# A fused decoder layer in one core: the up projection of blocks 1 to 3, hidden chunks 4 to 15, as seven half-size products instead of eight

## The reference, cut to what matters

```
def sq_relu_mlp(h, w_up, w_down):
    u = jax.nn.relu(h @ w_up)
    return (u * u) @ w_down
...
x = x + sq_relu_mlp(rms_norm(x, norm_mlp[i]), w_up[i], w_down[i])
return rms_norm(x, final_norm)
```

## Time and profile before

| | us |
|---|---|
| median of 3 runs | 2531.71 (2530.8 to 2531.89) |
| span of the profiled execution (first to last instruction) | 2527.2 |
| what the median is above that span | 4.5 |
| TensorE busy in the span | 2490.0 (99%) |
| VectorE busy | 1691.7 (67%) |
| ScalarE busy | 1247.7 (49%) |

### The profile page before, as it was taken

One profiled execution on the slowest core, in us unless ns is written; L12 is line 12 of the kernel. 1 busy time (PEld: TensorE's weight loads), 2 busy tenths in 40 slices (PEclk: granted clock), 3 DMA queues, 4 the chain that ended last, 5 costly groups with the idle time before them and its releaser, 6 DMA issues.

```text
span 2527.2 us, 31134 instructions
## 1 busy us (share of the span) xinstructions
PE 2490.0 (99%) x11724; PEld 2087.1 (83%) x11724; DVE 1691.7 (67%) x2473; ACT 1247.7 (49%) x1832; POOL 345.9 (14%) x328
## 2 busy tenths in 40 slices
PE   8999999999999999999999999999999999999998
PEld 7888887888788888888888888888888888888887
DVE  5677467566767786665566778656665687765566
ACT  5544354544554455455455445545455445554344
POOL 0034200000304320000110431000020143000000
PEclk9999999999999999999999999999999999999999
DMA  8522458555732143544442215354444213443443
GB/s 292 183 84 67 157 194 304 182 205 171 261 134 67 51 175 117 190 144 133 166 168 82 67 56 203 100 183 150 150 167 147 70 59 107 160 134 120 164 150 133
DMA packets 201681, 369.48 MB, mean 146 GB/s; under 512 B 8032, under 2 KB 120032, under 8 KB 192576
## 3 DMA queue, kind: packets, MB, share of 16 engines
q1 hardware_dynamic: 200912, 367.25, 43.0%
q10 hardware_dynamic: 624, 0.27, 0.0%
HBM read 336.03 MB, written 31.46 MB: 145 GB/s over the span
## 4 chain that ended last, share of the span: by engine, by line
PE 86%; DVE 5%; DMA 3%; ACT 2%; issue 2%; POOL 1%; DVEq 0%; SPq 0%; ACTq 0%; POOLq 0%
PE banks L2174 25%; PE banks L2175 25%; PE banks L2176 25%; PE banks L2348 3%; POOL queries L946 1%; PE banks L2387 1%; PE banks L2391 1%; PE banks L2327 1%; DVE w_lo L1527 1%; PE banks L2372 1%; PE banks L2304 1%; DMA xres<-in_x 1%; DMA raw<-w_out_mix 1%; DVE xres L1928 0%; DVE query_dec L1679 0%
## 5 line engine op out<-in xcount | busy, mean ns | idle before, releaser
L2174 PE MATMUL banks<-h_hi,w_hi 128*128 128x512 f32 (+1 forms) x1728 | 666.5, 386 | 3.3 <-issue 1.3
L2176 PE MATMUL banks<-h_hi,w_lo 128*128 128x512 f32 (+1 forms) x1728 | 659.0, 381 | 0.0
L2175 PE MATMUL banks<-h_lo,w_hi 128*128 128x512 f32 (+1 forms) x1728 | 659.0, 381 | 0.0
L1527 DVE TENSOR_TENSOR w_lo<-raw,w_hi 128x1024 fp32r<-128x1024 f32 x284 | 357.6, 1294 | 105.2 <-ACT w_hi L1030 97.6
L1520 DVE TENSOR_TENSOR w_lo<-raw,w_hi 128x2048 fp32r<-128x2048 f32 x122 | 292.6, 2398 | 149.2 <-ACT w_hi L1023 145.4
L1030 ACT ACTIVATE w_hi<-raw 128x1024 fp32r<-128x1024 f32 x248 | 253.9, 1053 | 279.3 <-PE banks L2174 93.0
L2174 PEld LDWEIGHTS banks<-h_hi,w_hi 128*128 128x128 f32 x1728 | 324.9, 188 | 66.2 <-issue 4.8
L2176 PEld LDWEIGHTS banks<-h_hi,w_lo 128*128 128x128 f32 x1728 | 324.8, 188 | 63.3
L2175 PEld LDWEIGHTS banks<-h_lo,w_hi 128*128 128x128 f32 x1728 | 325.0, 188 | 60.9
L2174 PE MATMUL banks<-w_hi,u_hi 128*128 128x512 f32 x896 | 350.9, 392 | 2.3 <-DVE w_lo L1527 1.8
L2176 PE MATMUL banks<-w_hi,u_lo 128*128 128x512 f32 x896 | 349.4, 390 | 0.0
(11 more groups left out here) (237 smaller groups left out, 3485.7 us busy)
## 6 DMA issues: line engine op xcount, KB each, us to landing
raw<-in_w_up SPq DMA_DIRECT2D x64, 1024.0 KB, 5.7
raw<-w_mix SPq DMA_DIRECT2D x64, 1024.0 KB, 4.7
raw<-in_gla_w_in SPq DMA_DIRECT2D x56, 1024.0 KB, 5.1
raw<-in_w_down SPq DMA_DIRECT2D x48, 1024.0 KB, 5.1
raw<-w_out_mix SPq DMA_DIRECT2D x24, 512.0 KB, 4.3
raw<-in_w_out SPq DMA_DIRECT2D x21, 512.0 KB, 3.7
xin<-in_w_down SPq DMA_DIRECT2D x10, 1024.0 KB, 5.1
w_mix<-xin SPq DMA_DIRECT2D x10, 1024.0 KB, 5.3
```

The lines of the kernel that those rows point to most:

```text
L1527: nc.vector.tensor_tensor(w_lo[:, i % 2, at], raw[:, i % 2, at], w_hi[:, i % 2, at].bitcast(F32), ALU.subtract).then_inc(lo_split.sem, 1)
L2174: after_chunk(pe.matmul(to, left[0], right[0], start=start, stop=False, skip_group_check=goes_on))
L2175: pe.matmul(to, left[0], right[1], start=False, stop=False, skip_group_check=goes_on)
L2176: return pe.matmul(to, left[1], right[0], start=False, stop=stop, skip_group_check=goes_on)
```

## The change

Block 0 keeps the order `MLP`. Blocks 1 to 3 get a list of their own, `LATE_MLP`: U0 to U3, down 0, U4 to U7, down 1, U8 to U11, down 2, U12 to U15, down 3. U0 to U3 (`PLAIN_UPS`) stay as they were; each of U4 to U15 becomes seven products of 4 blocks x 3 matmuls with 256 moving columns, issued as two steps, "up a" and "up b":

```
+LATE_UP_A = (("M1", A11, 0), ("M2", A12, 1), ("M6", S2, 2), ("M5", S1, 3))
+LATE_UP_B = (("M7", S3, 1), ("M3", S4, 0), ("M4", A22, 2))
+for _g in range(GROUPS):
+    for _c in range(DEPTH * _g, DEPTH * (_g + 1)):
+        LATE_MLP += [("up", _c)] if _c < PLAIN_UPS else [("up a", _c), ("up b", _c)]
+    LATE_MLP += [("down", _g, j) for j in range(len(PRODUCTS))]
+def late_bank(c, name):
+    return {"M2": 6, "M5": 1, "M3": 1}.get(name, 7 if c % 2 else 0)
```

TensorE. M1, M6, M7 and M4 of a chunk go on in one bank and M5, M3 in another, and ScalarE (`keep_part`) or VectorE (`add_part`) has to take the sum so far before the next product writes there:

```
+def late_up(s, c):
+    pe.wait_ge(*up_split_loaded[a % 2].at(n, late_parts_before(s)))
+    late_products(s, c, "M1", "M2")
...
+    wait_piece(s, 0)
+    late_products(s, c, "M6")
+    wait_piece(s, 1)
+    late_products(s, c, "M5")
...
+    wait_piece(s + 1, 0)
+    late_products(s + 1, c, "M7")
...
+    late_products(s + 1, c, "M3")
...
+    late_products(s + 1, c, "M4")
+# in late_products, before each product's 12 matmuls:
+        pe.wait_ge(*empty(n, ("up", c, name)))
```

ScalarE, in blocks 1 to 3 (its order for one late chunk, and at the start of a down group):

```
+def late_up(s, c):
+    if ahead is not None:
+        late_body(ahead)
+        corner(ahead)
+    keep_part(c, "M1")
+    if ahead is not None:
+        u_high(ahead, False)
+    late_split_hi(s + 1, 0) 
+    late_split_hi(s + 1, 1)
+    keep_part(c, "M6")
+    if ahead is not None:
+        u_high(ahead, True)
+    keep_part(c, "M5")
+    late_split_hi(s + 2, 0)
+    late_split_hi(s + 2, 1)
+    late_relu(c)
+def late_down(s, g, j):
+        late_body(c)
+        corner(c)
+        late_split_hi(s + 1, 0)
+        u_high(c, False)
...
```

VectorE, the same way:

```
+def late_up(s, c):
+        u_sums(ahead)
+    add_part(c, "M2")
+    late_split_lo(s + 1, 0)
+    late_split_lo(s + 1, 1)
+        u_low(ahead, False)
+        u_low(ahead, True)
+    add_part(c, "M7")
+    late_split_lo(s + 2, 0)
+    add_part(c, "M3")
+    late_split_lo(s + 2, 1)
+def late_down(s, g, j):
+        u_sums(c)
+        late_split_lo(s + 1, 0)
+        u_low(c, False)
+        late_split_lo(s + 1, 1)
+        u_low(c, True)
```

Block 0 makes what the late chunks load. For each of its up chunks 4 to 15, VectorE makes four sums of 512 columns (`up_mix`: four instructions, behind the split of that chunk), and SyncE stores them and the split weights that the late chunks use unchanged:

```
+def up_mix_store(c):
+    sp.wait_ge(up_mix_made, c - PLAIN_UPS + 1)
+    sp.dma_start(w_up_mix[:, c - PLAIN_UPS, 0:2, :], up_mix_t2_t1)
+    sp.dma_start(w_up_mix[:, c - PLAIN_UPS, 2:4, :], up_mix_t3_t4)
+def up_split_store(i, c):
+    for part, high_low in enumerate((w_hi, w_lo)):
...
...
+                    if s >= 2 and MLP[s - 2][0] == "up" and MLP[s - 2][1] >= PLAIN_UPS:
+                        up_mix_store(MLP[s - 2][1])
                     load(n, c_mlp + s, *mlp_source(s))
+                    if s >= 2 and MLP[s - 2][0] == "up" and MLP[s - 2][1] >= PLAIN_UPS:
+                        up_split_store(c_mlp + s - 2, MLP[s - 2][1])
...
+                        act.wait_ge(up_split_stored[slot], 64 * stored_ups(slot, s - 1))
```

More of the change, by code:

```diff
@@ L248, in block_uses @@
         yield from output_uses()
-    for what in MLP:
+    for what in MLP if plain else LATE_MLP:
         if what[0] == "up":
@@ L252, in block_uses @@
                 yield f, ("up", what[1], f)
+        elif what[0] in ("up a", "up b"):
+            for name, _, _ in LATE_UP_A if what[0] == "up a" else LATE_UP_B:
+                yield late_bank(what[1], name), ("up", what[1], name)
         else:
@@ L334, in __init__ @@
         self.mlp = C_OUT + out_chunks
-        self.chunks = self.mlp + len(MLP)
+        self.steps = MLP if plain else LATE_MLP
+        self.chunks = self.mlp + len(self.steps)
         self.uses = UseOrder(block_uses(plain))
@@ L717, in mlp_source, with late_weights, late_columns, stored_ups @@
             return wdown[:, 2 * DEPTH * g + row:2 * DEPTH * (g + 1):2, 512 * col:512 * (col + 1)], DEPTH
+        def late_weights(s):
+            what = LATE_MLP[s]
+            if what[0] == "up":
+                return wup[:, :, FCOLS * what[1]:FCOLS * (what[1] + 1)], KD
+            g, operand = what[1], PRODUCTS[what[2]][2]
+            if operand >= T1:
+                return w_mix[:, g, operand - T1, :, :], DEPTH
+            row, col = {B11: (0, 0), B21: (1, 0), B22: (1, 1)}[operand]
+            return wdown[:, 2 * DEPTH * g + row:2 * DEPTH * (g + 1):2, 512 * col:512 * (col + 1)], DEPTH
+        def late_columns(s, piece):
+            first = {"up a": 1024, "up b": 512}.get(LATE_MLP[s][0])
+            return slice(1024 * piece, 1024 * (piece + 1)) if first is None else \
+                slice(first + 512 * piece, first + 512 * (piece + 1))
+        def stored_ups(slot, steps):
+            return sum(MLP[t][0] == "up" and MLP[t][1] >= PLAIN_UPS and (FIRST.mlp + t) % 2 == slot for t in range(steps))
+        def late_parity(s):
+            return (OTHERS.mlp + s) % 2
+        def late_parts_before(s):
+            return sum(LATE_MLP[t][0] in ("up a", "up b") and late_parity(t) == late_parity(s) for t in range(s))
+        def ring(n):
+            return LATE_RING if n else RING
         def chunk_source(i):
@@ new lines, in first_mlp @@
+                            finish_u(after_up)
+                        if g == 1 and 1 <= j <= TILES:
+                            if j == 1:
+                                act.wait_ge(*xin_loaded.at(n, 0))
+                            square(1, j - 1, xin, n)
+                        if g == GROUPS - 1:
+                            if j == 0:
+                                act.wait_ge(*full(n, "next rstd"))
+                                nc.scalar.activation(rstd_rows, bank("next rstd"), ACT.Copy)\
+                                    .then_inc(bank_read[bank_of("next rstd")], 1)
+                            for k in NEXT_X_TILES.get(j, ()):
+                                next_x_high(k)
+                            if j == len(PRODUCTS) - 1:
+                                for t in range(2):
+                                    act.wait_ge(*read(n, ("down", g, "M2", t)))
+                                    square(2, t, xres, n)
@@ L1476, in _ @@
+                if n:
+                    late_mlp()
+                else:
+                    first_mlp()
                 for t in range(2, TILES):
@@ new lines, in first_mlp, with late_split_lo @@
+                        if g == GROUPS - 1:
+                            for k in NEXT_X_TILES.get(j, ()):
+                                next_x_low(k)
+                            if j == len(PRODUCTS) - 1:
+                                for t in range(2):
+                                    norm_ms(2, t)
+                def late_split_lo(s, piece):
+                    i, what = c_mlp + s, LATE_MLP[s]
+                    dve.wait_ge(*hi_split.at(n, PIECES * i + piece))
+                    at = late_columns(s, piece)
+                    nc.vector.tensor_tensor(w_lo[:, i % 2, at], raw[:, i % 2, at], w_hi[:, i % 2, at].bitcast(F32),
+                                            ALU.subtract).then_inc(lo_split.sem, 1)
@@ L2113, in final_scale, with late_mlp @@
+                def late_mlp():
+                    for s, what in enumerate(LATE_MLP):
+                        if what[0] == "up":
+                            plain_up(s, what[1])
+                        elif what[0] == "up a":
+                            late_up(s, what[1])
+                        elif what[0] == "down":
+                            late_down(s, *what[1:])
+                if n:
+                    late_mlp()
+                else:
+                    first_mlp()
                 def final_scale(t):
@@ L2689, in pe_block @@
                 first_up_chunk()
-                for s, what in enumerate(MLP):
+                for s, what in enumerate(mlp_steps):
                     if what[0] == "up":
```

567 lines of the change are left out of this document (435 added, 132 removed).

## The result

| | before | after |
|---|---|---|
| median of the runs, us | 2531.57 | 2553.73 (2552.59 to 2554.46) |
| span of the profiled execution, us | 2527.2 | 2550.8 |

The changed kernel is slower: 1.0089 times before, 95% interval 1.0075 to 1.0103, +22.2 us. The prediction had 2521.6 us in a range of 2510 to 2542: the time lies above the range, and where a small gain was forecast there is a loss.

A forecast was written before the change was run, and what follows sets the result against it. TensorE, busy 99% of the 2527.2 us span, bounds the kernel. With -28.8 (late chunks), 0 (other engines), +7.3 (down-group waits) and +11.4 (block 0) the span is 2517.1; plus 4.5 to the median, 2521.6 us, range 2510 to 2542.

The forecast's parts named there:

- Part 1: TensorE's work in late chunks of three blocks: 10.08 us for 10.88 in each of 36 chunks, -28.8 us.
- Part 2: Other engines in a late chunk: ScalarE's 7.9 and VectorE's 7.8 us fit in 10.08; cost taken 0.
- a sign of being wrong: Block 0's MLP over 20 us longer, late chunks above 10.2 us, or DMA waits into w_hi in blocks 1 to 3.
- The rival of ScalarE's chain: ScalarE overruns its 0.8 us spare, so M6 waits in 27 chunks, 2.7 us per 0.1 beyond; chance 0.11.
- Part 3: Down groups starting on the chunk just made: TensorE waits 0.85 us seven times and 0.45 three times, +7.3 us.
- M3 is added by T - 0.6: Before a down group, VectorE finishes adding M3 0.6 us before the chunk's matmuls end; leads to a 0.85 us wait.
- my upper bound, 15: Upper bound in us for the waits at down groups, taken as twice the forecast delay; lower bound 0.
- Part 4: Block 0's added sums and stores: 3.67 MB per up chunk at 364 GB/s make weights late, +11.4 us.
- the bound of 31: Slow bound for block 0's added cost in us, at 318 GB/s or 11.5 us a chunk.
- chunk 4's 3.0: Block 0, 395 to 410 us: 7.2 us of new queue bytes against 5.3 free; 3.0 us, chosen between 0 and 6.
- the stretch most like it: Block 0 row with 280 GB/s at a share of 0.77, taken as 364 GB/s at full share.
- The queue-bound rival: Block 0 becomes bound by the queue: 2541 us at 318 GB/s, shows as slower from 328 on; chance 0.23.

The follow-up runs named there:

- run 6: Changed kernel with product 1's first weight pieces split ahead of the work on u at down groups of blocks 1 to 3: 2544.64 us, ratio 1.0056.
- run 4: Changed kernel with block 0's split stores in pieces of 4 and 2 KB instead of 512 bytes, same bytes: 2543.28 us, ratio 1.0051.
- run 5: Changed kernel with SyncE in block 0 issuing the split store first, then the sums' store, then the load: 2544.52 us, ratio 1.0050.
- run 11: As run 8, with block 0's mixed down weights 12 and 13 two steps later, mixes 14 to 17 and x one step later: 2523.76 us, ratio 0.9976.
- run 8: Changed kernel with the orders of run 5 and run 6, plus block 0's load issued ahead of the sums' store: 2529.86 us, ratio 0.9996.

## Why the prediction was wrong

- **Part 1, -28.8 us: right.** Late chunks are 10.08 us apart. With the order of run 6, blocks 1 to 3 are 24.8 us shorter than before.
- **Part 2, nothing lost: right but for 1.3 us.** Of the nine groups of late chunks seven take 40.31 or 40.32 us. Two in block 2 take 40.60 and 41.27; 0.70 of that is one wait on the load of w_lo, in front of the matmul at 1883.24, of the kind that the prediction named as a sign of being wrong. The rival of ScalarE's chain falls: its waits in 27 chunks are not there.
- **Part 3, +7.3: mis-sized.** Without any new wait blocks 1 to 3 would take 1853.2 - 28.8 = 1824.4; they took 1840.1, so 15.7 more, of which 10.5 stand in the eight waits. The step that failed is "M3 is added by T - 0.6". VectorE was still splitting product 0's first half then, because those weights, issued at 1110.79, landed 7.7 us later, where I had 5.1; it added M3 at T + 0.1, the ReLU ended at T + 1.15 and not +0.3, and the waits in down 1, down 2 and the last down 3 are 1.1 to 1.5 us and not 0.85. In down 0 they are 0.24 and not 0.45, and in down 3 of block 1, where none was to be, there is one of 0.6. The rest of the 15.7 is what a wait costs beyond its length, and the 1.3 us of part 2: by the starts of the phases each down 1 and down 2 takes 1.4 to 1.9 us longer than before, each down 0 0.5, the three down 3 0.9, 0.0 and 2.0. The 15.7 are just above my upper bound, 15.
- **Part 4, +11.4: this is the step that decided.** It cost 36.7, above the bound of 31. Of the 25.3 us beyond the forecast, about 16 lie in the groups from up 5 on (24.5 measured, 8.4 forecast) and 8.7 at chunk 4. Two terms of the sum failed, the rate and chunk 4's 3.0, and so did the way of pricing a wait.
  - *The rate.* I took 364 GB/s from "the stretch most like it", but nothing in that stretch moves in 512-byte pieces. It was 327. With 11.2 us a chunk my own sums give 9.4, 9.0 and 2.8 us late for ups 5 to 8, 9 to 12 and 13 to 15; each group with its down group lost 10.0, 9.4 and 5.1. Run 4 tests the rate by itself, and there the three still lose 8.0, 4.8 and 3.4 where the forecast at 364 had 4.4, 4.0 and 0: the rate is a part of the miss, and that the sums at 327 come so close to the measured losses is in part luck. The queue-bound rival, which I gave 0.23, had this number (318) and its condition (slower below 328). I had written its argument down, "pieces of 512 bytes", and priced the other.
  - *Chunk 4.* It was to cost 3.0 and cost 11.7 (the phase of down 0). I had 5.3 us of the queue free there for 7.2 us of new bytes. The store that ScalarE waits for was issued last, but issuing it first (run 5) changes nothing here, 11.8 us, and neither do large pieces (run 4), 11.3. With the load ahead of the sums' store it is 9.6, and with the 4 MB of mixed weights, which nobody needed yet, moved out of the stretch (run 11) it is 3.5. Run 11 moves other transfers too, so the share of the mixed weights alone is not shown.
  - *The order.* I asked when a queue with so many bytes would be done, not which of them is waited for. By the medians runs 5 and 8 win 9 and 5 us by order alone; run 11, which takes bytes out of the crowd, wins 6.
  - *The clock.* A wait was priced at its length. The waits of 9.3, 5.0 and 2.4 us were each followed by a granted clock of 0.5 to 0.6 in the next 4 us, and that cost 5.7 us, 4.1 more than in the kernel before.
- **The sum.** 2517.1 forecast span; +25.3 in part 4 and +8.4 in parts 2 and 3 make the 2550.8. The median lies 2.9 us above that span, where I had added 4.5, the distance of the kernel before: no other execution on record has its time more than 3.0 above its span, so its profiled execution was a short one and the added term too large.
- Of what I said would be seen, the waits at down groups came, though the profile puts them down to ScalarE's split and not VectorE's, and ScalarE did wait for the store. But in block 0 TensorE stands in front of ups 8 and 12 (5.0 and 2.4 us), not for 3 to 5 us after down 1 and 2 have begun. "Block 0's MLP longer by over 20 us", the sign of being wrong, came too.

## What to carry to other kernels

When a change adds stores to a stretch, price them at the rate of a row with pieces of that size, and if there is none, let the slow bound be as likely as the fast one. Then list for each engine which landing it waits for, and issue in that order: what nobody waits for goes behind, also when it belongs to older work. And a wait of TensorE of several us costs more than its length, because the low clock can follow it (10.2 us of it in run 8's profiled execution, none in run 11's), so spreading the bytes until no single wait is long is worth trying beside removing them.

## What the runs showed of the hardware

- **Half clock after a wait.** In the changed kernel the clock was 0.50 after waits of 9.3 and 5.0 us and 0.60 after one of 2.4; in run 11, after one of 2.9, it was 1.00 (the row 411 to 414 above). The kernel before has the low clock too, after a wait of 1.84 us (a row of its timeline, then one of its windows):

```profile
407.83 0.47 PE L2174 MATMUL banks<-w_hi,u_hi 128*128 128x512 f32 x1 [1.84 <-DVE w_lo L1527]
408.00:412.00 4.00, 4.00 (x11) 3.11 (x11) 2.06 (x3) 0.00 (x0) 0.00 (x0) 0.57 1.01 296
```

  So the length of the last wait alone does not decide; what does, these runs don't show. The Trainium skill ("TensorE: Matmul & The Clock Gate", HAM oscillation) describes how waits on DMA throttle the clock anew each time. The trace agrees for the long waits: 0.50 after each of 9.3 and 5.0 us in the change, and of 7.2, 5.8 and 4.1 in run 8.
- **SyncE is held while it issues.** With the DMA engines busy (share 0.99 from 395 to 412), one DMA of 512-byte pieces took 6.34 us to issue, and all that stands behind it in the program is late by that, loads included. Large pieces do not end it: in run 4 the split stores took 0.7 us or less each in that place, but a load behind them 3.83.
- **Two overloads don't add.** The two parts cost 6.6 and 7.4 us alone and 35.0 together.
